# Roots and reciprocals of norms on one number per token, spread over the partitions by a product with diagonals

## What is computed

```python
def rms_norm(x, g):
    xf = x.astype(jnp.float32)
    var = jnp.mean(xf * xf, axis=-1, keepdims=True)
    return (xf * lax.rsqrt(var + EPS)).astype(x.dtype) * g
...
def layernorm(x, g, b):
    xf = x.astype(jnp.float32)
    mu = jnp.mean(xf, axis=-1, keepdims=True)
    var = jnp.mean(jnp.square(xf - mu), axis=-1, keepdims=True)
    y = (xf - mu) * lax.rsqrt(var + EPS)
    return (y * g.astype(jnp.float32) + b.astype(jnp.float32)).astype(x.dtype)
```

## Time and profile before

| | us |
|---|---|
| median of 3 runs (2518.5 to 2519.74) | 2519.7 |
| the profiled execution, its own time | 2521.25 |
| its span in the trace | 2518.5 |
| PE busy | 2461.1 |
| DVE busy | 1633.3 |
| ACT busy | 993.6 |

### The profile page before, as it was taken

How to read it: one execution, slowest core, us unless ns; L and a number is a source line. 1 busy time by engine, 2 the same in 40 slices (tenths; PEclk the granted TensorE clock), 3 DMA queues, 4 the chain that set the end, 5 groups by cost and what they waited for, 6 DMA issues and landing times.

```text
span 2518.5 us, 40380 instructions
## 1 busy us (share of the span) xinstructions
PE 2461.1 (98%) x14398; PEld 2147.0 (85%) x14398; DVE 1633.3 (65%) x2378; ACT 993.6 (39%) x1338; POOL 120.3 (5%) x138
## 2 busy tenths in 40 slices
PE   7999999999999998999999999989999999999998
PEld 2888888888888886888899999979999878888886
DVE  7567777777777775445555343468999975444346
ACT  4334444444444433333345222235455554322223
POOL 0011211111111100000000000000000000000000
PEclk9999999999999998999999999999999999999999
DMA  6212212122121232222222222222222222222222
GB/s 239 78 64 75 75 67 75 58 76 82 67 67 64 78 126 75 83 76 83 85 92 91 88 88 92 92 84 92 100 97 94 100 84 97 95 92 92 99 92 100
DMA packets 61983, 223.90 MB, mean 89 GB/s; under 512 B 6736, under 2 KB 8784, under 8 KB 61552
## 3 DMA queue, kind: packets, MB, share of 16 engines
q1 hardware_dynamic: 58992, 211.08, 24.7%
q0 software_dynamic: 2944, 12.19, 1.4%
HBM read 221.15 MB, written 2.10 MB: 89 GB/s over the span
## 4 chain that ended last, share of the span: by engine, by line
PE 93%; DVE 4%; ACT 1%; issue 1%; DMA 1%; ACTq 0%; DVEq 0%; SPq 0%
PE ps L489 81%; PE ps L663 4%; PE ps L685 1%; PE ps L546 1%; DMA ada_raw<-in_ada_weights_dram 1%; PE ps L676 1%; PE ps L704 1%; PE ps L650 1%; PE ps L695 1%; PE ps L696 1%; PE ps L697 1%; ACT w_hi L1060 1%; DVE w_lo L1603 1%; PE ps L633 0%; DVE n_sq L1622 0%
## 5 line engine op out<-in xcount | busy, mean ns | idle before, releaser
L1060 ACT ACTIVATE w_hi<-w_raw 128x1024 fp32r<-128x1024 f32 (+1 forms) x360 | 377.8, 1049 | 922.5 <-PE ps L489 913.7
L1603 DVE TENSOR_TENSOR w_lo<-w_raw,w_hi 128x1024 fp32r<-128x1024 f32 (+1 forms) x360 | 435.3, 1209 | 214.4 <-ACT w_hi L1060 212.2
L489 PE MATMUL ps<-n_hi,w_hi 128*128 128x512 f32 (+1 forms) x992 | 320.5, 355 | 11.9 <-DVE n_lo L1630 8.5
L489 PE MATMUL ps<-n_lo,w_hi 128*128 128x512 f32 (+1 forms) x992 | 319.6, 354 | 0.0
L489 PE MATMUL ps<-n_hi,w_lo 128*128 128x512 f32 (+1 forms) x992 | 318.0, 352 | 0.0
L489 PE MATMUL ps<-h_hi,w_hi 128*128 128x512 f32 x640 | 266.5, 416 | 4.8 <-DVE h_lo L1735 3.1
L489 PE MATMUL ps<-h_hi,w_lo 128*128 128x512 f32 x640 | 251.2, 393 | 0.0
L489 PE MATMUL ps<-h_lo,w_hi 128*128 128x512 f32 x640 | 250.4, 391 | 0.0
L489 PEld LDWEIGHTS ps<-n_hi,w_hi 128*128 128x128 f32 x992 | 174.5, 189 | 45.4 <-issue 11.0
L489 PEld LDWEIGHTS ps<-n_hi,w_lo 128*128 128x128 f32 x992 | 174.6, 189 | 25.9
L489 PEld LDWEIGHTS ps<-n_lo,w_hi 128*128 128x128 f32 x992 | 174.4, 189 | 26.1 <-issue 0.2
(11 more groups left out here) (367 smaller groups left out, 4963.8 us busy)
## 6 DMA issues: line engine op xcount, KB each, us to landing
w_raw<-in_weights_dram SPq DMA_DIRECT2D x376, 512.0 KB, 3.3
ada_raw<-in_ada_weights_dram SPq DMA_DIRECT2D x4, 2048.0 KB, 22.4
gate_raw<-in_gate_weights_dram POOLq DMA_DIRECT2D x16, 512.0 KB, 3.6
x<-in_x_dram SPq DMA_DIRECT2D x1, 2048.0 KB, 14.6
x<-in_x_dram POOLq DMA_DIRECT2D x1, 2048.0 KB, 9.9
out_dram<-fin SPq DMA_DIRECT2D x16, 128.0 KB, 1.9
xc<-in_ctx_dram SPq DMA_DIRECT2D x1, 1024.0 KB, 21.2
masks<-in_masks_dram POOLq DMA_DIRECT2D x1, 512.0 KB, 4.8
```

Source lines behind the costliest of these rows:

```text
L489: last = nc.tensor.matmul(o, w, xp, start=start and n == 0, stop=stop and n == 2)
L1060: run(w_hi[:, s, 0:n], w_raw[:, s, 0:n], ACT.Copy).then_inc(hi_ready[s], 1)
L1603: tt(w_lo[:, s, 0:n], w_raw[:, s, 0:n], w_hi[:, s, 0:n].bitcast(F32), ALU.subtract).then_inc(lo_ready[s], 1)
```

## The change

At the four places, the mean is computed the other way round. The sum of squares is now the stationary operand, one tile of 128 tokens after the other, and two columns of `ones_d` are the moving one (`token_means`). The mean of a token so lies on one partition: 4 pairs of columns for 512 tokens, 5 for 528 (the last tile overlaps its neighbour), 2 for a half of 256. ACT takes the root of 4, 5 or 2 columns into `inv`, and DVE the reciprocal of these (`inverse`). To bring the numbers back to all partitions, DVE multiplies the identity by them, times 128, which gives a row of diagonal matrices ([128, tokens]; in `h_fold`, `n2["tmp"][:, 1]` or `odd_taps`, which is the same place), and PE multiplies `ones_h` by these diagonals (`spread`). The result stays in PSUM, and the multiplications by the reciprocal read it there.

In N1, a second identical product goes to bank 5, and ACT copies it to `n1["sq"]`, ahead of the roundings of the 8 slices, for the use in `fold`. In the layer norm, DVE makes the diagonals ahead of the gate of row 5, and PE's spread stands behind the fifth tile of row 6. In NOUT, ACT takes the root of the first half one square earlier; DVE makes the diagonals of that half ahead of one addition, and finishes two slices ahead of the last half row instead of behind it; PE's spread for that half stands in the middle of the last half row (after three of its six tiles).

The diff, with the helpers that it adds:

```diff
+        inv = g.take("inv", [P, 8])
...
-        NFIN, NOUT = norm_sems("nfin", "mean", "root", "hi", "lo"), norm_sems("nout", "sum", "mean", "root", "lo")
-        NF1, NF2 = [norm_sems(t, "sum", "mean", "root", "hi", "lo") for t in ("nf1", "nf2")]
+        NFIN, NOUT = norm_sems("nfin", "mean", "root"), norm_sems("nout", "sum", "mean", "root", "lo")
+        NF1, NF2 = [norm_sems(t, "mean", "root", "hi", "lo") for t in ("nf1", "nf2")]
+        inverse_ready, spread_done = sem("inverse_ready"), sem("spread_done")
...
+        def token_tiles(n):
+            return [*range(0, n - P + 1, P), *([n - P] if n % P else [])]
+        def over_two(bank, n):
+            return ps[:, bank:bank + 2].rearrange("p a b -> p (a b)")[:, 0:n]
+        def roots_in(bank, n):
+            return ps[:, bank, 0:2 * n:2]
...
+            def token_means(bank, src, n):
+                for t, a in enumerate(token_tiles(n)):
+                    last = nc.tensor.matmul(ps[:, bank, 2 * t:2 * t + 2], src[:, a:a + P], ones_d[:, 0:2],
+                                            start=True, stop=True)
+                return last
+            def spread(count, bank, diagonals, n):
+                pe.wait_ge(inverse_ready, count)
+                m_ = min(n, T)
+                last = nc.tensor.matmul(ps[:, bank, 0:m_], ones_h[:], diagonals[:, 0:m_], start=True, stop=True)
+                if n > T:
+                    last = nc.tensor.matmul(ps[:, bank + 1, 0:n - T], ones_h[:], diagonals[:, T:n],
+                                            start=True, stop=True)
+                last.then_inc(spread_done, 1)
...
-            mean(N1, T, n1["sum"][:, 0])
+            pe.wait_ge(N1["sum"], 1)
+            token_means(6, n1["sum"][:, 0], T).then_inc(N1["mean"], 1)
+            spread(1, 7, h_fold[:], T)
+            nc.tensor.matmul(ps[:, 5], ones_h[:], h_fold[:], start=True, stop=True).then_inc(N1["mean"], 1)
...
             def mean_of_half(N, n, half):
                 c = n // 2
                 pe.wait_ge(N["sum"], half + 1)
-                nc.tensor.matmul(ps[:, 6 + half, 0:c], ones_d[:], n2["sum"][:, 0, half * c:(half + 1) * c],
-                                 start=True, stop=True).then_inc(N["mean"], 1)
+                token_means(6 + half, n2["sum"][:, 0, half * c:(half + 1) * c], c).then_inc(N["mean"], 1)
+            def spread_half(half):
+                c = HALF_T
+                spread(4 + half, 4 + half, n2["tmp"][:, 1, half * c:(half + 1) * c], c)
...
-                        last = tiles(s[a], [ps[:, 2 * a + half, 0:n // 2]], xs, range(count), True, True)
+                        o, split = [ps[:, 2 * a + half, 0:n // 2]], count
+                        if half and a:
+                            split = count // 2
+                            tiles(s[a], o, xs, range(split), True, False)
+                            spread_half(0)
+                        first = split % count
+                        last = tiles(s[a], o, xs, range(first, count), not first, True, first)
                         last.then_inc(w_used[s[a]] if half else done, 1)
                         if half and a == 0:
                             mean_of_half(N, n, 0)
...
-            mean(NMIX, TM, n2["sum"][:, 0])
+            pe.wait_ge(NMIX["sum"], 1)
+            token_means(6, n2["sum"][:, 0], TM).then_inc(NMIX["mean"], 1)
+            spread(2, 4, n2["tmp"][:, 1], TM)
...
-            def rnn_out(ks, aside=None):
...
                     first = 0
-                    if aside and n == 0:
-                        first = 2
-                        tiles(s, o, xs, range(first), True, False)
+                    for at, aside in asides.items() if n == 0 else ():
+                        tiles(s, o, xs, range(first, at), not first, False, first)
+                        first = at
                         aside()
                     tiles(s, o, xs, range(first, KD), not first, True, first).then_inc(w_used[s], 1)
...
             rnn_out((4, 5))
-            rnn_out((6, 7), lambda: ln_mean(7, 2, centred_sq[:, 0]))
+            def ln_variance():
+                pe.wait_ge(ln_sum, 2)
+                token_means(7, centred_sq[:, 0], T).then_inc(ln_pe, 1)
+            rnn_out((6, 7), {2: ln_variance, 5: lambda: spread(3, 6, odd_taps, T)})
...
             mean_of_half(NOUT, T, 1)
+            spread_half(1)
...
             fetch_root()
             act.wait_ge(N1["sum"], 1)
-            root(N1, ps[:, 6], n1["sq"][:, 0])
+            root(N1, roots_in(6, TT), inv[:, 0:TT])
+            act.wait_ge(N1["mean"], 2)
+            run(n1["sq"][:, 0], ps[:, 5], ACT.Copy).then_inc(N1["root"], 1)
             norm_hi(N1, lambda k: nf_hi[:, k], lambda k: n1["tmp"][:, k % 2], lambda k: ada1[:, k, 0:1])
...
-                root(N, ps[:, 6:8, 0:HALF], halves(n2["sq"][:, 0]))
+                root(N, roots_in(6, TT + 1), inv[:, 0:TT + 1])
                 norm_hi(N, lambda k: n_hi[:, k], lambda k: n2["tmp"][:, k % 2], lambda k: zero[:])
...
             def half_root(N, n, half):
-                c = n // 2
                 act.wait_ge(N["mean"], half + 1)
-                run(n2["sq"][:, 0, half * c:(half + 1) * c], ps[:, 6 + half, 0:c], ACT.Sqrt, bias=eps[:]
+                run(inv[:, half * TT:half * TT + FOLD], roots_in(6 + half, FOLD), ACT.Sqrt, bias=eps[:]
                     ).then_inc(N["root"], 1)
...
             act.wait_ge(ln_pe, 2)
-            run(n2["sq"][:, 0, 0:T], ps[:, 7], ACT.Sqrt, bias=eps[:]).then_inc(ln_act, 1)
+            run(inv[:, 0:TT], roots_in(7, TT), ACT.Sqrt, bias=eps[:]).then_inc(ln_act, 1)
             run(warm[:], zero[:], ACT.Silu)
...
             half_square(RD2, T, 0, 0)
             half_square(RD2, T, 1, 0)
+            half_root(NOUT, T, 0)
             half_square(RD2, T, 0, 1)
-            half_root(NOUT, T, 0)
             half_square(RD2, T, 1, 1)
             half_root(NOUT, T, 1)
...
+            def inverse(count, n, diagonals, at=0):
+                m_, rest = n // P, n % P
+                tiles_ = len(token_tiles(n))
+                own.link(v.reciprocal(inv[:, at:at + tiles_], inv[:, at:at + tiles_]))
+                last = stt(diagonals[:, 0:m_ * P].rearrange("p (t s) -> p t s", s=P),
+                           ident[:].unsqueeze(1).broadcast_to([P, m_, P]), float(P),
+                           inv[:, at:at + m_].unsqueeze(2).broadcast_to([P, m_, P]), ALU.mult, ALU.mult)
+                if rest:
+                    last = ts(diagonals[:, m_ * P:n], ident[:, P - rest:P], inv[:, at + m_:at + m_ + 1], float(P),
+                              ALU.mult, ALU.mult)
+                last.then_inc(inverse_ready, 1)
+            def norm_apply(N, count, n, diagonals, src, gain, shift, tmp, rt_, hi, lo):
                 dve.wait_ge(N["root"], 1)
-                own.link(v.reciprocal(rt_, rt_))
+                inverse(count, n, diagonals)
+                dve.wait_ge(spread_done, count)
                 for k in range(KD + 1):
                     if k < KD:
...
-            norm_apply(N1, lambda k: x1[:, k], lambda k: scale[:, 2, k:k + 1], lambda k: ada1[:, k, 0:1],
-                       lambda k: n1["tmp"][:, k % 2], n1["sq"][:, 0], lambda k: nf_hi[:, k], lambda k: nf_lo[:, k])
+            norm_apply(N1, 1, T, h_fold[:], lambda k: x1[:, k], lambda k: scale[:, 2, k:k + 1], lambda k: ada1[:, k, 0:1],
+                       lambda k: n1["tmp"][:, k % 2], ps[:, 7], lambda k: nf_hi[:, k], lambda k: nf_lo[:, k])
...
             after(0)
+            dve.wait_ge(N1["root"], 2)
             fold(0)
...
             def block_norm(N, name):
-                norm_apply(N, lambda k: hb[:, k], lambda k: col(name, k), lambda k: zero[:],
-                           lambda k: n2["tmp"][:, k % 2], n2["sq"][:, 0], lambda k: n_hi[:, k], lambda k: n_lo[:, k])
+                norm_apply(N, 2, TM, n2["tmp"][:, 1], lambda k: hb[:, k], lambda k: col(name, k), lambda k: zero[:],
+                           lambda k: n2["tmp"][:, k % 2], over_two(4, TM), lambda k: n_hi[:, k], lambda k: n_lo[:, k])
...
             def half_inverse(N, n, half):
                 c = slice(half * (n // 2), (half + 1) * (n // 2))
                 dve.wait_ge(N["root"], half + 1)
-                own.link(v.reciprocal(n2["sq"][:, 0, c], n2["sq"][:, 0, c]))
+                inverse(4 + half, n // 2, n2["tmp"][:, 1, c], half * TT)
...
-            lroot = n2["sq"][:, 0, 0:T]
+            lroot = ps[:, 6]
...
             tt(total, total, other, ALU.add).then_inc(ln_sum, 1)
             gated(0, 4)
             after(1)
+            dve.wait_ge(ln_act, KD + 1)
+            inverse(3, T, odd_taps)
             gated(1, 5)
             st.leave(1)
-            dve.wait_ge(ln_act, KD + 1)
-            own.link(v.reciprocal(lroot, lroot))
+            dve.wait_ge(spread_done, 3)
             st.enter(0, 2)
...
             def finished(half, ks):
                 c, x = slice(half * HALF_T, (half + 1) * HALF_T), META + half * HALF_T
```

(19 more changed lines are left out.)

## The result

| | before | after |
|---|---|---|
| median of 7 runs, us | 2518.89 (2517.84 to 2519.80) | 2526.91 (2525.96 to 2528.06) |
| profiled execution, us | 2521.25 | 2526.09 |
| its span, us | 2518.5 | 2524.4 |

The ratio is 1.0032, interval 1.0023 to 1.0041: 8 us slower, where 2.7 us faster was forecast: 2517.0, with a range of 2513.6 to 2519.6.

What follows compares the result with a forecast made beforehand. PE was taken as the bound, busy 2461.1 of 2518.5 us, so norms could gain little beyond its waits. +0.57 - 0.46 - 1.45 - 1.35 = -2.7 us, from a median of 2519.7, gave 2517.0 us, range 2513.6 to 2519.6.

Steps and rivals of the forecast that it cites:

- The slower rival: In the new means, loads do not overlap with products: up to 0.36 us a pass, +8.1, 2525.1 us; chance 0.06.
- N1: First `lo` +0.57 us later: the shorter reciprocal's gain is eaten by diagonals, spread and the copy's detour.
- NMIX: `tmp` 0 0.46 us earlier, with ACT's table work hiding the mean and no copy in ACT's way.
- layer norm: DVE's slices start 1.45 us earlier; PE has some 0.85 more to do but still waits for them.
- NOUT: At the kernel's end, -1.35 us: DVE's multiplications 1.2 earlier and stores 0.15, with the second spread at half clock.
- that rival (0.15): In the layer norm PE becomes the bound: +0.85 us instead of -1.45, so 2519.3 us; chance 0.15.
- the rival with 0.20: PE's clock stays up through the spreads: N1 -1.1, NMIX -1.4, the end -1.8, together -5.8 us, 2513.9; chance 0.20.
- PSUM operands: Rival: each of 32 slices reading the spread from PSUM takes 0.06 us longer, +1.9, 2518.9 us; chance 0.07.

Runs made afterwards that it cites:

- b_pad32: The kernel before plus one unused tile of 32 bytes per partition where the change takes `inv`; 2530.40 us, ratio 1.0045 to before.
- a_slot: The changed kernel with `inv` inside the 32 bytes that `unused` occupies anyway, so no tile moves; 2515.35 us, ratio 0.9989 to before.
- a_slot_n1: As a_slot, but with N1 given back its old chain; 2513.80 us, ratio 0.9983 to before.
- a_align: The changed kernel with `inv` placed as in a_slot and the wide rows of b_align; 2505.92 us, ratio 0.9951 to before.
- b_align: The kernel before with rows of `n_hi`, `n_lo`, `hid_hi`, `hid_lo` 2304 instead of 2112 bytes apart, their 512-column products at 128 modulo 256; 2510.02 us, ratio 0.9967.
- a_inv64: The changed kernel with `inv` widened from 32 to 64 bytes per partition; 2518.61 us, ratio 0.9997 to before.
- b_pad64: The kernel before plus an unused tile of 64 bytes per partition where the change takes `inv`; 2520.23 us, ratio 1.0005 to before.
- b_head128: The kernel before plus 128 unused bytes ahead of the first tile, so stationary and moving tiles shift together; 2516.98 us in one execution, before 2517.64.

## Why the prediction was wrong

**The step that failed** is a term that the sum puts at nothing without a reason. It prices instructions and waits place by place; the new tile `inv` has no term, and the sum is taken from a span in which all products that the diff does not touch stay as they are. They did not, since `inv` moves every tile behind it by 32 bytes. In place of nothing the runs showed: +11.8 us of median and +12.8 of span for the 32 bytes alone (b_pad32 against before), and +11.3 us of span for the same 32 bytes in the changed kernel (2524.4 against a_slot's 2513.1), of which some 1.5 is a fall of the clock that a_slot's trace lacks. None of the rivals looked outside the norms, so the true outcome had no chance of its own. The slower rival, two-column passes paid in full, had the right sign and with 2525.1 nearly the right number, by luck: from the rows above a pass took (1.05 - 0.25) / 7 = 0.11 us at N1 and as much at NMIX, not 0.36.

**The terms of the sum held.**

| | forecast | traced, after against before | the same, other pairs |
|---|---|---|---|
| N1 | +0.57 | +0.36 | +0.75 (a_slot, a_slot_n1) |
| NMIX | -0.46 | -0.46 | -0.45 (a_slot, before) |
| layer norm | -1.45 | -1.5 | -1.41 (a_align, b_align) |
| NOUT | -1.35 | -1.84 | -1.82 (a_align, b_align) |
| sum | -2.7 | -3.4 | -2.9 |

For NMIX both numbers are from the mean's start to the first product. For the layer norm the last column runs from the first product over `a` to the first over `mg`. The medians of the four pairs of kernels with the same placement all have this sign: a_slot -2.9 against before, the change -3.5 against b_pad32, a_align -4.1 against b_align, and a_inv64 -1.6 against b_pad64. Only the first pair has an interval of its ratio, and it is barely clear of 1 (0.9998); so the sign is well supported, and the size rests on the timelines.

- **N1.** `tmp` 0 came 1.0 us earlier and the first `lo` 0.36 later, with the copy between. The means cost 1.05, 0.09 less than forecast, and the spread 1.86 to the start of the second product; the copy took 0.60 where I had 0.69.
- **NMIX** as forecast in this pair. It varies with where the clock falls: from the mean's start to the first product it is 8.2 or 8.9 us with the old chain (8.9 in b_pad32 and b_align, where the clock fell ahead of the mean), and 7.7 to 8.6 with the new one (8.6 in a_inv64).
- **Layer norm.** DVE 1.5 earlier, PE still waits for the slices (1.2 us), so PE did not become the bound, and that rival (0.15) falls.
- **NOUT** was undersized by 0.5. I had let the second spread run at half clock, 1.05; it ran at full clock, 0.70, and ended under the first multiplications, which went through in one piece (ten in 4.10). The traces differ here: in a_slot the clock had fallen, the spread took 1.22, and the same place gave -1.4.
- **Clock.** It fell ahead of the spreads at N1 and NMIX, so there the rival with 0.20 falls; at the end the clock held, and its price for the end, -1.8, is what came.
- **PSUM operands.** Two multiplications of 128x512 took 1.41 with the spread in PSUM and 1.41 with it in SBUF; ten of 128x256 took 4.10 and 4.05. By the rule of the Trainium skill that the prediction cites (Perfetto Trace Analysis, Optimizing Scalar/DVE Operations) they would be some 65 ns apart each; the trace does not agree.

A page that would have spoken against looking at placement: the Trainium skill, TensorE: Matmul & The Clock Gate, section "Step-by-step: what each phase is for", says that the engine reads the streaming and the stationary operand through two independent ports, and that loading the next weights takes no bandwidth from the running product. Taken alone that gives no reason for the distance of two tiles to matter. The runs show that it does: with the same instructions the products lie 227 or 233 ns apart, by how far the moving tile is from the stationary one. Whether the loads of the stationary tile are what costs it, no run shows, so the page's sentence is neither borne out nor refuted.

What stays open: why. That the two reads meet in the memory would fit b_head128 and the pairs with every other engine idle, but no run separates the load of the stationary tile from the product, or `w_hi` and `w_lo` from the other tiles ahead of the pad. `mg` at a shift of 64 (233.3) stands out from `y` and `g` (229) at the same phase, so the phase is not the whole rule.

## What to carry to other kernels

A new tile is part of the change even if nobody waits for it: print the start addresses of all tiles before and after, and if any tile moved, compare one untouched product in both traces from start to start before anything else is explained. To judge a change of the algorithm, put new tiles where nothing moves (in the padding of a small one, or at the end). Where back-to-back products bound a kernel, try the distance between moving and stationary tiles in steps of 32 bytes up to 256, and the pitch of the rows; here that gave over three times what the rewritten norms did. Then look at PE's waits again: a faster PE met DVE's weight cutting, which took back some 3 us.
